# Weight loads, bank waits and emission order in a two-layer diffusion-transformer kernel

## The chip, the cores and the metric

The kernel runs on one core of a Trainium2 chip. A core has TensorE (matrix products, PE in the profile), VectorE (DVE), ScalarE (ACT), GpSimd (POOL), SyncE (SP, which here only issues DMAs) and 16 DMA engines. The engines run their own instruction streams in order and meet only at semaphores. The metric is the device time of one execution in microseconds (us), lower is better; the time before is 1897.44 us, the median of 3 runs (1891.87 to 1897.72).

## The reference

Two layers of a block with three attention branches in parallel, over 512 tokens `x` and 256 context tokens `ctx` of 1024 features; only `x` is returned, so the last layer computes no context output.

```python
def hybrid_layer(x, ctx, c, c_ctx, lw, pos, update_ctx):
    mod_x = silu(c) @ ada_w + ada_b                 # shift, scale, gate
    mod_c = silu(c_ctx) @ ada_w + ada_b
    h  = rmsnorm(x, norm_w) * (1 + scale) + shift   # hc likewise
    p = h @ w_in                                    # 1024 -> 6816 columns
    k_m, v_m, k_s, v_s, k_a, v_a = project_kv(...)  # latents, rope, norms
    q_m, q_s, q_a, z_m, z_s, z_a, g = project_q(...)
    o_m, o_s, o_a = dense MLA, window and dense axial attention, 8 heads each
    y = sum over b of sigmoid(g_b) * ((o_b * silu(z_b)) @ w_o_b)
    x = x + gate * (y @ w_out)                      # ctx likewise if update_ctx

for l in range(2): x, ctx = hybrid_layer(...)
return rmsnorm(x, final_norm_w)
```

## The kernel before

Everything is float32. A product is made of three passes of rounded parts: high x high, high x low, low x high. So each weight chunk (up to 128 x 1024, 512 KB) is loaded by SP into a slot `w_raw`, ScalarE writes `w_hi` (line 1498) and GpSimd writes the rest `w_lo` over the raw data (line 1703); then TensorE may use it. Activations are split likewise: an event `H` on ScalarE writes the high part, an event `L` on VectorE the low part.

A planner, `schedule()`, writes one list of events by hand-made rules, and every engine walks that list in order and takes its own part of each event. A projection is a `group`: an event `G` (the matmuls, line 1273, which alternate between two PSUM banks `acc[0]` and `acc[1]`), an event `E` (reading the bank, on ScalarE, VectorE or both) and, where asked for, `H` and `L`, which the planner puts into a list `later` with a lag; `flush()` empties it at once. A group may start only when the bank's last group has been read. `chunk()` gives each weight the slot that was used longest ago among `usable` slots: three (`TIGHT`) during attention, four (`ROOMY`) elsewhere. The fourth shares memory with attention buffers, so SP waits with it for all value products issued so far (`slot_pv`). The order of the calls of `chunk()` is SP's order of issue, and a wait of SP holds all that is behind it. `split_ahead()` decides where the event `W` of a chunk (both splits) goes.

The stages of a layer, in order: (1) the modulation: rows of `ada_w` are summed by VectorE (`AD`) or, for layer 0's scale, by TensorE with four-row products (`AF`, line 1291); `AC` and `AT` turn the scale row into columns, `VT` transposes the small vectors, `XQ`, `XN`, `XT`, `XM` square, normalise, transpose and modulate the tokens. (2) The latents `ak`, `ckv`, `cq`, `kr` and their sums of squares (`statb`, `statq`). (3) The attention: a loop over pairs of query tiles and heads, with scores into `wide`, softmax, transposes into `ptp`, value products into `pv`; a queue of other groups (the next heads' `mla_head`, the `z` and `y` tiles, queries and keys of the next branch) fills its gaps. (4) Merge: 8 feature tiles, each a gate projection (`g`, then a `tanh` on ScalarE) and the last branch's output projection (`y`), with the rows of `ada_w` for the gate and the next shift in between (`due` says how many after which tile). (5) `wout`: 4 column parts times the token tiles, 24 products of 256 columns each, over all 8 feature tiles.

Ropes use two shared buffers: `swapped` (VectorE shuffles into it, GpSimd multiplies and adds) and `rot`, the result. Before the change each rope's `E` (waits in lines 1785 to 1788) waits until every earlier low part is written, and the planner flushes before it. In `wout` the wait of a group is for all low parts of `y` (`y_ready`, line 795). In `statb` and `statq` TensorE waits for `ev_a=n["ev_a"]`, all reads of ScalarE up to then.

## Time and profile before

| | before |
|---|---|
| median of 3 runs | 1897.44 us (1891.87 to 1897.72) |
| the profiled execution | 1901.16 us |
| its span, first to last instruction | 1899.1 us |
| mean granted TensorE clock | 0.961 |
| TensorE busy | 1744.3 us (92%) |
| VectorE, ScalarE, GpSimd busy | 1086.3, 1048.3, 517.7 us |
| HBM read, mean rate | 121.49 MB, 66 GB/s |

How to read it: the profile is one execution. Its views used here are the page (busy time by engine), the table of waits (for each pair of waiting and releasing operation the idle time in total, how often, and the longest), the timeline (instructions in order of time; in brackets the idle time before an instruction and what ended it) and the table by stretch, in which PEclk is the clock granted to TensorE as a share of 2.4 GHz. A line such as L1273 is the line of the kernel; `acc<-h_hi,w_hi` names what is written and read.

### The profile page before, as it was taken

To read this page: it belongs to the slowest core of one execution; us is meant where nothing else is said; L and a number is where in the kernel's file an instruction comes from. 1 tells how busy PE (TensorE), PEld (TensorE's weight loads), DVE (VectorE), ACT (ScalarE), POOL (GpSimd) and SP (SyncE) were. 2 spreads that over 40 slices of the span, in tenths; PEclk is the share of its full clock that TensorE was granted. 3 is DMA by queue.
4 is the path that set the end of the run, shared out by engine and by line. 5 is a ranking of instruction groups with operands and counts; after the bars stand their busy time and mean duration, and the time that the engine had idled before them with its cause. 6 is when DMAs were issued, how large, how long until landed. Compare 5 with 4: busy or idle time off the path is not lost. (4 is left out here: it accounts for less than half of the span.)

```text
span 1899.1 us, 26967 instructions
## 1 busy us (share of the span) xinstructions
PE 1744.3 (92%) x10544; PEld 1523.4 (80%) x10544; DVE 1086.3 (57%) x2183; ACT 1048.3 (55%) x1915; POOL 517.7 (27%) x296
## 2 busy tenths in 40 slices
PE   7989988999998999998999998978899979999997
PEld 3867877889997889887889976867778867888777
DVE  5533776665555565554756643666565555665534
ACT  3434776666665676754221523766566656776322
POOL 1513212122222222222222432322133222332342
PEclk8998999999999999999999998989999998999899
DMA  8111011011111111114454321111112221211542
GB/s 307 47 24 27 24 32 34 22 40 46 51 46 45 30 49 40 42 37 150 118 165 140 112 60 30 33 30 34 34 45 74 54 61 40 56 51 51 183 133 89
DMA packets 174302, 127.41 MB, mean 67 GB/s; under 512 B 21533, under 2 KB 163423, under 8 KB 174176
## 3 DMA queue, kind: packets, MB, share of 16 engines
q1 hardware_dynamic: 170018, 113.27, 21.1%
q10 hardware_dynamic: 2878, 8.24, 1.2%
q0 software_dynamic: 1280, 4.20, 0.7%
q8 instruction: 83, 1.36, 0.3%
q14 instruction: 43, 0.35, 0.1%
HBM read 121.49 MB, written 4.19 MB: 66 GB/s over the span
## 5 line engine op out<-in xcount | busy, mean ns | idle before, releaser
L1703 POOL TENSOR_TENSOR w_lo<-w_raw,w_hi 128x1024 fp32r<-128x1024 f32 (+4 forms) x188 | 382.5, 2038 | 1217.2 <-ACT w_hi L1498 1216.9
L1273 PE MATMUL acc<-h_hi,w_hi 128*128 128x512 f32 (+2 forms) x1320 | 470.4, 357 | 27.2 <-DVE rot L1798 10.3
L1273 PE MATMUL acc<-h_hi,w_lo 128*128 128x512 f32 (+2 forms) x1320 | 466.1, 354 | 0.0
L1273 PE MATMUL acc<-h_lo,w_hi 128*128 128x512 f32 (+2 forms) x1320 | 462.2, 354 | 0.3 <-POOL h_lo L1741 0.3
L1594 ACT ACTIVATE pt<-ptp 128x512 fp32r<-128x512 f32 (+3 forms) x312 | 166.1, 563 | 271.5 <-PE ptp L1345 270.9
L1887 DVE TENSOR_REDUCE nmax<-wide 128x1 f32<-128x768 f32 (+3 forms) x240 | 189.9, 791 | 208.3 <-PE wide L1325 206.7
L1273 PEld LDWEIGHTS acc<-h_hi,w_hi 128*128 128x128 f32 (+1 forms) x1320 | 251.5, 191 | 68.1 <-issue 16.6
L1273 PEld LDWEIGHTS acc<-h_hi,w_lo 128*128 128x128 f32 (+1 forms) x1320 | 251.1, 190 | 35.0
L1273 PEld LDWEIGHTS acc<-h_lo,w_hi 128*128 128x128 f32 (+1 forms) x1320 | 248.9, 190 | 36.2 <-POOL h_lo L1741 0.5
L1912 DVE TENSOR_TENSOR pt<-ptp,pt 128x512 fp32r<-128x512 f32 (+3 forms) x312 | 192.1, 641 | 54.4 <-ACT pt L1594 54.3
L1586 ACT ACTIVATE e<-e,einv 128x768 f32<-128x768 f32 (+3 forms) x240 | 193.3, 805 | 47.3 <-DVE einv L1904 46.9
L1498 ACT ACTIVATE w_hi<-w_raw 128x1024 fp32r<-128x1024 f32 (+4 forms) x188 | 168.4, 900 | 89.0 <-DMA w_raw<-in_w_out 62.2
L1345 PE MATMUL ptp<-ident,e 128*128 128x128 f32 x1152 | 166.5, 279 | 1.1 <-ACT e L1586 1.1
L1579 ACT ACTIVATE e<-wide,nbias,rq 128x768 f32<-128x768 f32 x160 | 144.9, 906 | 27.1 <-DVE nbias L1893 24.0
L1345 PEld LDWEIGHTS ptp<-ident,e 128*128 128x128 f32 x1152 | 135.1, 143 | 3.2 <-ACT e L1586 1.9
L1325 PE MATMUL wide<-k_s,q_s 128*128 128x256 f32 (+2 forms) x576 | 127.1, 337 | 2.3 <-DVE q_s L1452 1.7
L1358 PE MATMUL pv<-pt,v_s 128*128 128x256 f32 (+1 forms) x384 | 100.3, 288 | 22.6 <-DVE pt L1912 13.6
L1273 PE MATMUL acc<-og_hi,w_hi 128*128 128x512 f32 (+1 forms) x288 | 106.0, 368 | 7.2 <-ACT th_x L1538 7.2
L1273 PE MATMUL acc<-og_lo,w_hi 128*128 128x512 f32 (+1 forms) x288 | 105.3, 366 | 0.0
L1273 PE MATMUL acc<-og_hi,w_lo 128*128 128x512 f32 (+1 forms) x288 | 105.2, 365 | 0.0
L1358 PEld LDWEIGHTS pv<-pt,v_s 128*128 128x128 f32 x384 | 73.5, 191 | 34.1 <-DVE pt L1912 28.8
L1359 PE MATMUL pv<-pt,v_s 128*128 128x256 f32 (+1 forms) x384 | 99.0, 285 | 0.0
(206 smaller groups left out, 3144.4 us busy)
## 6 DMA issues: line engine op xcount, KB each, us to landing
w_raw<-in_w_in SPq DMA_DIRECT2D x102, 512.0 KB, 4.0
w_raw<-in_ada_w SPq DMA_DIRECT2D x48, 512.0 KB, 6.1
w_raw<-in_w_out SPq DMA_DIRECT2D x16, 512.0 KB, 3.5
w_raw<-in_w_o_mla SPq DMA_DIRECT2D x16, 256.0 KB, 2.8
w_raw<-in_w_o_swa SPq DMA_DIRECT2D x16, 256.0 KB, 2.9
w_raw<-in_w_o_ax SPq DMA_DIRECT2D x16, 256.0 KB, 2.8
w_raw<-in_mla_w_uq SPq DMA_DIRECT2D x16, 144.0 KB, 2.4
xres<-in_x SPq DMA_DIRECT2D x2, 1024.0 KB, 16.1
```

What stands on the lines that cost most here:

```text
L1273: ins = nc.tensor.matmul(dst, lhs, rhs, start=first, stop=last)
L1325: ins = nc.tensor.matmul(wide[:, c0:c0 + nk], lhs, rhs, start=(i == 0), stop=(i == len(pairs) - 1 and not masks))
L1345: ins = nc.tensor.transpose(ptp_of(t)[:, b:b + P], e_of(u, c0, c0 + P), ident[:, :])
L1358: nc.tensor.matmul(dst, v_of(pa, kt), pt_of(t, 0)[:, b], start=t["first"] and i == 0, stop=False)
L1359: ins = nc.tensor.matmul(dst, v_of(pa, kt), pt_of(t, 1)[:, b], start=False, stop=t["last"] and i == len(t["blocks"]) - 1)
L1498: nc.scalar.activation(w_hi[s][:, 0:k], w_raw[s][:, 0:k], ACT.Copy).then_inc(w_hi_ready, 1)
L1579: nc.scalar.activation(e_of(u), wide[:, u["lo"]:u["lo"] + u["width"]], ACT.Exp, bias=nbias[:, r:r + 1], scale=scale, accum_out=esum[:, r:r ...
L1586: nc.scalar.activation(e_of(u), e_of(u), ACT.Copy, scale=einv[:, r:r + 1]).then_inc(norm_act, 1)
L1594: nc.scalar.activation(pt_of(t, 0), ptp_of(t), ACT.Copy).then_inc(pt_hi_ready, 1)
L1703: nc.gpsimd.tensor_tensor(w_lo[s][:, 0:k], w_raw[s][:, 0:k], f(w_hi[s][:, 0:k]), ALU.subtract).then_inc(w_lo_ready, 1)
L1887: link(nc.vector.tensor_reduce(nmax[:, r:r + 1], wide[:, u["lo"]:u["lo"] + u["width"]], AX.X, ALU.max, negate=True))
L1912: nc.vector.tensor_tensor(pt_of(t, 1), ptp_of(t), f(pt_of(t, 0)), ALU.subtract).then_inc(pt_lo_ready, 1)
```

## The change

It changes orders and waits; no arithmetic is added but three products that only keep TensorE at work.

- First modulation: the 16 chunks are loaded in another order (shift rows ahead of scale rows), the copy of the small vectors on VectorE (`VC`) moves behind the sixth row, squares and norms of the first two tiles by one row, the first tile's transposes and the shift sums go ahead of `AT`, the second tile's behind it, and three products `KW` are added. The product into `acc[1]` follows the real ones in `AF`.
- Latents: the sums wait for their own squares only, and stand between the query latents 0 and 1 with the rope key before query latent 2; ScalarE's wait in `statb` is for the sum two before.
- Ropes: query heads of the MLA branch (`qm`) and `ak` no longer use `rot`; `qm` writes into `q_f`, the float32 view of its own low part. A rope waits on VectorE only for the low part of the last user of `rot`, and there is a flush only if that one is still due.
- `mla_head` for heads 2, 4, 6: key, value, key, value, query instead of key, key, query, value, value.
- Merge: the chunks of tile t+1 are asked for ahead of the rows behind tile t, and gate chunk 1 is placed while only three slots are usable.
- `wout`: a group waits for feature tile 6 of its own token group, and for tile 7 ahead of its last three products.

```diff
--- before.py
+++ after.py
...
     chunk_last, chunk_at, held, last_used, th_last = {}, {}, [0], [0], {0: None, 1: None}
+    rot_last = [None]
     turn, usable, now, holding = [0], [ROOMY], [0.0], [False]
...
             if g.get("roped"):
-                flush()
-                g["rope_prev"] = (n["rope"], n["l"])
+                if kind not in ("qm", "ak"):
+                    if rot_last[0] is not None and "low_n" not in rot_last[0]:
+                        flush()
+                    g["rot_before"] = rot_last[0]
+                    rot_last[0] = g
+                g["rope_prev"] = n["rope"]
                 n["rope"] += 1
...
         sums, scale = [], []
-        for k in range(KD):
-            sums.append(shift_row(k))
-            scale.append(chunk("adr", 0, 1, k, (0, 1), slot=FIRST[KD + k]))
-            whole.add(scale[-1])
-            used[scale[-1]] = 0
+        for third in (0, 0, 0, 1, 0, 0, 1, 0, 1, 0, 1, 0, 1, 1, 1, 1):
+            if third == 0:
+                sums.append(shift_row(len(sums)))
+            else:
+                scale.append(chunk("adr", 0, 1, len(scale), (0, 1), slot=FIRST[KD + len(scale)]))
+                whole.add(scale[-1])
+                used[scale[-1]] = 0
         early = chunk("win", 0, C_AK, P), chunk("win", 0, C_CKV, P)
...
                 emit("VT")
-            if k == KD // 2 + 1:
+            if k == KD - 3:
+                emit("VC")
+            if k == KD - 2:
                 for tt in (a, b):
...
         emit("AC")
-        for tt in (a, b):
-            turn_rows(tt)
+        turn_rows(a)
+        run_all(shift_sums())
         emit("AT")
+        turn_rows(b)
+        for i in range(2):
+            emit("KW", c=scale[0])
         emit("W", c=early[0])
...
         load_table("s")
-        run_all(shift_sums())
         for tt in (c, d):
...
         turn_rows(c)
+        emit("KW", c=scale[0])
         modulate_rows(b)
...
-    def y_tile(l, b, t, og):
+    def y_tile(l, b, t, og, slots=None):
         branch = BRANCHES[b]
-        cg, cy = chunk("win", l, C_G[branch] + t * P, P), chunk("wo", l, b, t)
+        cg = chunk("win", l, C_G[branch] + t * P, P)
+        usable[0] = slots or usable[0]
+        cy = chunk("wo", l, b, t)
         gates = {tg: project("g", l, cg, tg, branch=branch, t=t, dve=False) for tg in token_groups(l)}
-        ys = [project("y", l, cy, tg, src="og", k=KO, branch=branch, t=t, of=gates[tg], hl=(b == 2), act=False,
+        ys = y_of[l, b, t] = [project("y", l, cy, tg, src="og", k=KO, branch=branch, t=t, of=gates[tg], hl=(b == 2), act=False,
                       needs=lambda: dict(l_done=og[branch])) for tg in token_groups(l)]
...
-    row_of = {}
+    row_of, y_of = {}, {}
...
         go(project("ak", l, ck, "c", roped=False, oldest=ck))
+        squares_ak = n["ev_a"]
         for t in range(KKV):
             go(project("ckv", l, cks[t], "c", t=t))
+        squares_ckv = n["ev_a"]
         load_table("m")
-        for tg in ("x", "c"):
-            go(group("statb", mode="statb", l=l, tg=tg, what="ak", tiles=1, nsum=HD,
-                     needs=lambda: dict(ev_a=n["ev_a"]), rope_done=ropes_ak))
-        for t in range(KQ):
-            c = chunk("win", l, C_CQ + t * P, P)
-            for tg in tgs:
-                go(project("cq", l, c, tg, what="cq", t=t))
-        for tg in ("x", "c"):
-            go(group("statb", mode="statb", l=l, tg=tg, what="ckv", hl=True, tiles=KKV, nsum=KV_RANK, needs=lambda: dict(ev_a=n["ev_a"])))
+
+        def key_sums(tg):
+            go(group("statb", mode="statb", l=l, tg=tg, what="ak", tiles=1, nsum=HD, needs=lambda: dict(ev_a=squares_ak), rope_done=ropes_ak))
+
+        def latent_sums(tg):
+            go(group("statb", mode="statb", l=l, tg=tg, what="ckv", hl=True, tiles=KKV, nsum=KV_RANK, needs=lambda: dict(ev_a=squares_ckv)))
+
+        def query_latents(t, tg, held={}):
+            if tg == "x":
+                held[l, t] = chunk("win", l, C_CQ + t * P, P)
+            if tg in tgs:
+                go(project("cq", l, held[l, t], tg, what="cq", t=t))
+
+        key_sums("x")
+        key_sums("c")
+        query_latents(0, "x")
+        latent_sums("x")
+        query_latents(0, "c")
+        query_latents(1, "x")
+        latent_sums("c")
+        query_latents(1, "c")
         c = chunk("win", l, C_KR, MLA_ROPE)
...
             go(project("kr", l, c, tg, m=MLA_ROPE, width=MLA_ROPE, what="kr", **roped(tg)))
+        for t in range(2, KQ):
+            for tg in tgs:
+                query_latents(t, tg)
         run_all(z_tile(l, 0, 0, zs, og))
...
                 qg += head_q(h + 1, chunk("mq", l, h + 1), 0)
-            return [s for g in (qg + kg + vg if h == 0 else kg + qg + vg) for s in g["steps"]]
+            if h % 2 == 0 and h:
+                return [s for g in (kg[0], vg[0], kg[1], vg[1], *qg) for s in g["steps"]]
+            return [s for g in qg + kg + vg for s in g["steps"]]
...
         sums_at = {3: gate_sums, 6: shift_sums} if l + 1 < LAYERS else {4: gate_sums}
+        tile = y_tile(l, 2, 0, og)
         for t in range(KD):
...
                 merge += step_of(lambda: scale_table(l + 1, V_AXK))
-            merge += y_tile(l, 2, t, og)
-            if t == 0:
-                usable[0] = ROOMY
+            merge += tile
+            if t + 1 < KD:
+                tile = y_tile(l, 2, t + 1, og, slots=ROOMY)
             if t in sums_at:
...
-        y_ready = n["l"]
+        y_low = {(t, g["tg"]): g["low_n"] for t in range(KD) for g in y_of[l, 2, t]}
         gates = n["free"]
...
                     run_all(side_sums())
+                tg = "x" if tt >= TT_CTX else "c"
                 g = go(group("wout", chunk_ids=cc, act=False, cost=cost_of(256, 3 * KD), mode="wout", l=l, j=j, tt=tt, xl=n["xl"],
-                             gates=gates, needs=lambda: dict(l_done=y_ready)))
+                             gates=gates, needs=lambda: dict(l_done=y_low[KD - 2, tg], last=y_low[KD - 1, tg])))
                 if sides and n["xr"] % 2 == 0:
...
     q_m = [shared(f"q_m{i}", [P, 2, TOK], R, at) for i, at in enumerate((51200, 57344, 118784))]
+    q_f = [shared(f"q_f{i}", [P, 2, TOK], F, at) for i, at in enumerate((51200, 57344, 118784))]
     k_m = [shared(f"k_m{i}", [P, 2, TOK], R, at) for i, at in enumerate((63488, 69632, 18432))]
...
                     for i, (dst, lhs, rhs, first, last) in enumerate(mm[a:b]):
+                        if mode == "wout" and a + i == 3 * (KD - 1):
+                            if new(l_done, need["last"]):
+                                pe.wait_ge(l_done, need["last"])
                         if g.get("low_last") and i == 2 * (b - a) // 3:
...
                         pe.wait_ge(raw_load[slot_of[c]], loads[c])
-                    if k < KD - 1:
-                        nc.tensor.matmul(acc[1][0:4, :], cs_n[:, k, :], w_raw[slot_of[c]][:, 0:512], start=True, stop=True)
                     for half in range(2):
...
                         ins.then_inc(af_done, 1)
+                    if k < KD - 1:
+                        nc.tensor.matmul(acc[1][0:4, :], cs_n[:, k, :], w_raw[slot_of[c]][:, 0:512], start=True, stop=True)
+                elif ev == "KW":
+                    if new(row_copied, 1):
+                        pe.wait_ge(row_copied, 1)
+                    nc.tensor.matmul(first_sums(1), cs_n[:, 0, :], w_raw[slot_of[e["c"]]][:, 0:512], start=True, stop=True)
                 elif ev == "AT":
...
+        def rope_out(g, rows):
+
+            if g["kind"] == "ak":
+                return lf[rows, cols("x")]
+            if g["kind"] == "qm":
+                return q_f[g["head"] % 3][rows, 1, cols("x")]
+            return rot[rows, :]
+
         def pieces(g):
...
                 q = q_m[g["head"] % 3]
-                return [(q[0:MLA_K, 0, c], q[0:MLA_K, 1, c], src[0:MLA_K, 0:N])], None
+                got = rope_out(g, slice(0, MLA_K)) if g["roped"] else src[0:MLA_K, 0:N]
+                return [(q[0:MLA_K, 0, c], q[0:MLA_K, 1, c], got)], None
             if what == "km":
...
                     elif kind == "statb":
-                        if new(stat_done, g["stat"] - 1):
-                            act.wait_ge(stat_done, g["stat"] - 1)
+                        if g["stat"] > 2:
+                            if new(stat_done, g["stat"] - 2):
+                                act.wait_ge(stat_done, g["stat"] - 2)
                         ins = nc.scalar.activation(lat_r[:, cols(g["tg"])], src[:, 0:N], ACT.Sqrt, scale=1.0 / g["nsum"], bias=eps_col[:, 0:1])
...
                     rows = slice(0, g["m"]) if g["kind"] != "kr" else slice(MLA_NOPE, MLA_K)
-                    dst = lf[rows, cols("x")] if g["kind"] == "ak" else rot[rows, :]
+                    dst = rope_out(g, rows)
                     if g["kind"] == "kr":
...
-                        if new(rope_done, g["rope_prev"][0]):
-                            dve.wait_ge(rope_done, g["rope_prev"][0])
-                        if new(l_done, g["rope_prev"][1]):
-                            dve.wait_ge(l_done, g["rope_prev"][1])
+                        if new(rope_done, g["rope_prev"]):
+                            dve.wait_ge(rope_done, g["rope_prev"])
+                        if g.get("rot_before") is not None:
+                            if new(l_done, g["rot_before"]["low_n"]):
+                                dve.wait_ge(l_done, g["rot_before"]["low_n"])
                         if new(tab_load, 32 * g["tab"]):
...
                         flip = 8 if kind in ("kr", "qm") else 16
-                        dst = lf[rows, cols("x")] if kind == "ak" else rot[rows, :]
+                        dst = rope_out(g, rows)
                         nc.vector.stream_shuffle(swapped[rows, :], src[pr, 0:N], [i ^ flip for i in range(32)])
...
                     ins.then_inc(ada_used, 1)
-                elif ev == "VT":
+                elif ev == "VC":
                     if new(vec_done, 2):
...
```

## Rows read from the trace of the kernel before

**Rows 1.** The page, first part: busy time and share of each engine.

```profile
PE 1744.3 (92%) x10544; PEld 1523.4 (80%) x10544; DVE 1086.3 (57%) x2183; ACT 1048.3 (55%) x1915; POOL 517.7 (27%) x296
```

**Rows 2.** Waits of TensorE: who waited for whom: total, times, longest (us).

```profile
PE pv L1358 <- DVE pt L1912: 29.9, 26, 3.1
PE pv L1358 <- DVE o_half L1919: 23.9, 16, 2.5
PE acc L1273 <- POOL w_lo L1703: 16.3, 6, 5.9
PE acc L1273 <- DVE rot L1798: 15.5, 6, 4.6
PE acc L1273 <- DVE k_m L1452: 11.9, 6, 3.3
PE acc L1273 <- ACT th_x L1538: 8.3, 5, 3.8
PE acc L1273 <- DVE y_lo L1875: 5.2, 2, 3.2
PE acc L1273 <- ACT lat_r L1520: 3.1, 4, 0.8
PE acc L1273 <- ACT cq_hi L1445: 2.1, 2, 1.3
```

**Rows 3.** Busy time by stretch: length, engines, granted clock (PEclk), DMA share, GB/s.

```profile
897.57:903.03 5.46, 5.46 (x13) 4.30 (x14) 0.00 (x0) 0.65 (x2) 3.05 (x2) 0.50 0.74 248
1773.61:1780.86 7.25, 7.25 (x24) 5.75 (x25) 5.77 (x4) 1.69 (x2) 4.03 (x2) 0.76 0.65 208
124.76:131.98 7.22, 7.22 (x24) 5.71 (x25) 1.80 (x4) 2.43 (x3) 3.26 (x3) 0.76 0.05 13
1004.51:1008.92 4.41, 4.41 (x26) 4.41 (x27) 0.00 (x0) 0.00 (x0) 0.00 (x0) 0.66 0.99 333
1839.57:1845.08 5.51, 5.51 (x26) 5.51 (x27) 0.00 (x0) 1.22 (x2) 4.70 (x2) 0.50 0.24 95
36.00:42.00 6.00, 6.00 (x32) 6.00 (x31) 0.00 (x0) 1.46 (x4) 3.53 (x3) 0.54 0.85 213
```

**Rows 4.** Timeline: start, length, operation; in brackets idle before it and releaser.

```profile
895.88 1.06 ACT L1498 ACTIVATE w_hi<-w_raw 128x1024 fp32r<-128x1024 f32 x1 [6.98 <-DMA w_raw<-in_w_in]
...
1750.46 0.69 DVE L1843 TENSOR_TENSOR y<-y,th_x 128x512 f32<-128x512 f32 x1
...
1773.61 0.56 PE L1273 MATMUL acc<-h_hi,w_hi 128*128 128x512 f32 x1 [2.84 <-POOL w_lo L1703]
```

**Rows 5.** Timeline of POOL, end of layer 1's Merge.

```profile
1835.21 2.37 POOL L1703 TENSOR_TENSOR w_lo<-w_raw,w_hi 128x1024 fp32r<-128x1024 f32 x1 [1.73 <-ACT w_hi L1498]
```

**Rows 6.** Timeline of VectorE, layer 1's first query latent.

```profile
1122.21 0.74 DVE L1454 SCALAR_TENSOR_TENSOR cq_lo<-acc,vec,cq_hi 128x512 fp32r<-128x512 f32 x1
```

**Rows 7.** Timeline of POOL and VectorE, layer 1's first query ropes.

```profile
1164.32 1.29 POOL L1732 TENSOR_TENSOR rot<-rot,swapped 96x512 f32<-96x512 f32 x1
...
1167.16 0.73 DVE L1797 STREAM_SHUFFLE swapped<-acc 96x512 f32<-96x512 f32 x1
```

**Rows 8.** Timeline of VectorE, key pair of layer 1's head 6.

```profile
1286.56 2.27 DVE L1452 TENSOR_TENSOR k_m<-acc,k_m 64x512 fp32r<-64x512 f32 x4 [1.14 <-ACT k_m L1443]
```

**Rows 9.** Timeline of VectorE, ScalarE and TensorE, first modulation.

```profile
18.77 0.21 DVE L1950 COPY vec<-acc 128x54 f32<-128x54 f32 x1 [3.31 <-PE acc L1283]
...
21.59 1.06 ACT L1653 ACTIVATE h_lo<-xres 128x1024 fp32r<-128x1024 f32 x1 [8.71 <-DMA xres<-in_x]
...
24.17 0.59 PE L1291 MATMUL acc<-w_raw,cs_n 128*4 128x512 f32 x1 [0.19 <-DMA w_raw<-in_ada_w]
...
29.44 1.28 DVE L1945 SCALAR_TENSOR_TENSOR w_raw<-w_raw,cs_n,wide 128x1024 f32<-128x1024 f32 x1
...
33.93 1.94 PE L1303 MATMUL pv<-sel,a_row 5*128 5x2 f32 x16
```

**Rows 10.** Timeline of VectorE, first tile of layer 1's Merge.

```profile
1772.44 1.66 DVE L1843 TENSOR_TENSOR y<-y,th_x 128x512 f32<-128x512 f32 x1
```

## The prediction

> **What bounds the kernel now.** I read the page first, then the table of what TensorE waited for, then the timeline of each engine around its longest waits, then the granted clock of the stretches behind them. TensorE is busy for 1744 of 1899 us [rows 1]. So a gain must come out of two places: the 155 us in which it stands still, and the time it works at the lower of its two clock levels. The table of waits [rows 2] sorts the first: 53.8 us are the value product waiting for VectorE inside the attention chain (its first two rows), and no edit here touches those. The others that the change can touch are waits of `acc` groups (line 1273): on POOL's split of a weight (16.3 us, of which one at 1773.61 counts here), on VectorE's rope output `rot` (15.5), on `k_m` (11.9), on ScalarE's `th_x` (8.3), on `y_lo` (5.2), on `lat_r` (3.1) and on `cq_hi` (2.1).
>
> **What a stop costs beyond itself.** Behind a long stop the granted clock is 0.50, which is the 1.2 GHz level, for some five us [rows 3]: 5.46 us after the stop of 3.8 at the start of layer 0's Merge, 5.51 after the stop of 3.2 at the end of layer 1's. I count the loss as (1 - clock) x length: 2.7, 1.7, 1.7, 1.5 and 2.8 us for the first five rows in their order. Taking a stop away should give its clock loss back too, since TensorE worked at 1.00 before these stops; I keep the case that it does not as a rival.
>
> **Merge's start.** Before the change gate chunk 1 takes the fourth weight slot, so SP waits with it for the last value product, and issues it behind rows of 512 KB (two or three). ScalarE meets its split ahead of the `tanh` of gate 0 in its own order and stands there for 6.98 us until the data has landed [rows 4], and TensorE waits 3.8 us for that `tanh` [rows 2]. In layer 1 the same load makes TensorE wait 2.84 us for POOL's `w_lo` [rows 4]. With the change this chunk takes one of three slots; its last user is the final `wo` chunk of the branch before, done some 7 us (layer 0) and 11 us (layer 1) before the attention ends. In layer 1 VectorE adds that last `y` at 1750.46 [rows 4]. The load starts there, with an idle queue, and both splits are done under gate 0. Gain: 3.8 + 2.84 of stops and 2.7 + 1.7 of clock, **11.0 us**. Bounds: 6.6 (stops alone) and 11.0. What is late next: `wo` chunk 1 in the fourth slot, now ahead of the rows, wanted a whole tile later; nothing. SP now also waits for `y` of tile t before it issues the rows behind `wo` t+2; VectorE wants these after tile t+1, 8.8 us (layer 1) to 13 us (layer 0) later.
>
> **Merge's end.** `wout` now waits for feature tile 6 and takes tile 7 only at its last three products of 24. Layer 0: the weights are ready, the stop is 5.2 - 3.2 = 2.0 us [rows 2] and goes whole, with 1.5 of clock [rows 3]. Layer 1: POOL's split of the second `wout` chunk ends at 1835.21 + 2.37 = 1837.6 [rows 5], TensorE began at 1839.57, so only 2.0 of 3.2 go; the remaining 1.2 us stop is short, and I take the clock loss of 2.8 as gone. Sum **8.3 us**, bounds 4.0 and 8.3. Its last-tile wait is covered: 21 products at 0.12 us are 2.5 us, tile 7's low part comes 2 us after the start. Behind it the later `wout` weights are loaded when a pair of slots comes free, so they shift along with the products.
>
> **Latents between sums.** The sums now wait for their own squares, not for the newest of all: `lat_r` 3.1 and `cq_hi` 2.1 go, and so do two of the `rot` stops (2.9 and 2.8, the z tile behind the rope key), because two query groups now lie between [rows 2]. That is 10.9 us, and 1.7 of clock at 124.76 [rows 3]. It adds stops: the next query group wants the bank that VectorE clears with `cq_lo`, and VectorE is behind with the reciprocals of the key sums; in layer 1 it comes to the first `cq_lo` at 1122.21 [rows 6], where the group that wants the bank would be ready about 1 us before. The same stands a second time behind the latent sum. Two per layer, each 0.8 to 1.0 us: minus 3.7. Net **8.9 us**, bounds 4 and 12.
>
> **Ropes of the queries.** Head 1's rope no longer waits for head 0's low part, only for POOL to have done with `swapped`. Layer 1: POOL ends at 1165.61, VectorE began at 1167.16 [rows 7]: 1.5 us; the same in layer 0. **3.0 us**; between 0 and 7, since layer 1 works at 0.50 for some 8 us behind this place and might not.
>
> **Value products between pair keys.** Of the 11.9 us on `k_m`, 10.1 are the four stops of heads 4 and 6 in both layers: the query wants the bank of the first key product while ScalarE copies four pieces and VectorE takes 2.27 us for its four [rows 8]. With 18 small value products (2.1 us) between the two key groups, about 0.5 us of each stop is left, so up to 8 go, and 3 of clock. But ScalarE and VectorE are each busy near three quarters here with work that isn't less, and the two top rows of [rows 2] follow at once. I take half of the stops and half of the clock: **6.5 us**, bounds minus 4 and 12.
>
> **The start.** VectorE stands 3.31 us for the transposed vectors [rows 9]; the copy moves behind the sixth row and this goes. But x now lands three chunks later. Two chunks lie between its landing (21.59) and that of scale chunk 5 (24.17) [rows 9], 1.3 us each: so x at 25.5, and its statistics, which need 4.3 us, at 29.8. VectorE began its last row at 29.44 [rows 9], would now be there at 26.1, and stands until 29.8: all of it is given back. Scale chunk 5 lands at 26.8, so TensorE's last passes end 2.6 us later than before, of which 0.9 fall into a stop that was there. One tile's transposes and the row turn (1.94) [rows 9], 2.9 us together, no longer stand ahead of the shift sums: they begin 1.1 us earlier, but the row turn follows them, and the modulation waits for it: 0.8 us late in all, at the same clock. The stretch from 36 to 42, in which these sums run, was granted 0.54 [rows 3], 2.8 us lost; as the passes end later, most of it may run at 1.00. I take plus 1.0, bounds minus 1.5 and 2. The rest of this stage is a chain over POOL and shifts with it. The three products that keep TensorE busy lie in its waits for `x_mod`.
>
> **Sum**: 11.0 + 8.3 + 8.9 + 3.0 + 6.5 + 1.0 = 38.7 us. The profiled execution took 1901.16 us (2.1 more than its span), 3.7 above the median of the three runs, 1897.44, and above all of them. I set the sum against it, 1901.2 - 38.7 = 1862.5, and say **1862**; against the median it would be 1858.7.
>
> **A rule that speaks against it.** VectorE's add of `y` and `th_x`, both in SBUF, took 1.66 us beside a POOL split [rows 10] and 0.69 without one [rows 4]. The Trainium skill (SBUF — State Buffer, Who interferes with whom) says that a VectorE instruction with two SBUF inputs contends with a GpSimd instruction that reads SBUF; the trace agrees. The change moves the split of gate chunk 1 beside `og_lo`, four such instructions, which end 2.0 us before TensorE needs them in layer 1. If each grew by the 1.0 us of the two rows, `og_lo` would be 2 us late and Merge's start worth 9 instead of 11: 1864.5.
>
> **Rivals.**
> - The clock stays low after the shortened stops (or falls elsewhere). Then only stops are won: 6.6 + 4.0 + 7.2 + 3.0 + 5.0 + 0 = 25.8, **1875**. For it: layer 0's stop of only 2.0 us is followed by 0.66 too. Against: 1.00 wherever groups follow without a stop. 0.12.
> - The attention takes it back: the key stops were cover for ScalarE and VectorE, and the value product waits instead. The pairs cost 4 instead of giving 6.5: **1873**. 0.12.
> - More is won: pairs 12, the ropes with their clock 7, the start 2: **1852**. 0.18.
> - The gate chunk is not early, because its slot's last user ends late or ScalarE meets its split elsewhere: minus 11, **1873.5**. 0.05.
> - Slower: the rows in Merge. They are issued behind a wait for `y`, and VectorE, which works in order, would hold `th_x` and with it every tile. It decides once three rows take longer than one tile, 8.8 us, to land; at 1.3 us a chunk [rows 9] three take 4. Were it so, some 4 us on 14 tiles: 56 us against the 38.7 won: **1918**. 0.03.
>
> The forecast as worked out has 0.50, within 8 us. All rivals but the last are faster by over 0.3% (5.7 us, about what a measurement of this kernel tells from no change); only several of them together reach no change, and I give that 0.03. So faster 0.94, same 0.03, slower 0.03. **Range**: 1848 to 1880, from "more is won" to two of the smaller rivals at once; outside on either side about 0.1.
>
> **What would show it.** In the table of waits: `th_x` down by 3.8, `y_lo` gone or below 1.5 in all, `lat_r` and `cq_hi` gone, new short waits on `cq_lo`, `k_m` below 4; ScalarE's split of gate chunk 1 ahead of the `tanh` without a DMA wait; the clock 1.00 over the first groups of Merge and of `wout`. It is wrong if the rows on `pt` and `o_half` grow by more than 5 us, if x's statistics do not hold VectorE at the seventh row, or if SP's rows land after VectorE asks for them.

## The result, and the profile after

The changed kernel took 1868.24 us (median of four, 1863.98 to 1868.50), the kernel before 1897.58 (median of four): ratio 0.9833 [0.9814, 0.9851], so 29.3 us less. The forecast was 1862, in a range of 1848 to 1880. The profiled execution of the changed kernel was the fastest of its four, 1863.98 us with a span of 1861.9; between the two profiled executions lie 37.2 us, against 38.7 forecast. I show below that this agreement is partly luck.

The table of waits of TensorE after (line waited for: total us, times, longest), which answers [rows 2]:

```profile
engine line waited for: us in total, times, longest us
PE pv L1401 <- DVE pt L1966: 29.7, 27, 3.1
PE pv L1401 <- DVE o_half L1973: 23.6, 16, 2.4
PE acc L1312 <- POOL w_lo L1756: 14.3, 5, 5.9
...
PE acc L1312 <- DVE k_m L1504: 4.9, 3, 2.2
PE acc L1312 <- ACT th_x L1591: 4.0, 4, 1.7
PE acc L1312 <- DVE rot L1852: 4.0, 1, 4.0
PE acc L1312 <- DVE cq_lo L1506: 3.9, 4, 1.7
PE pv L1330 <- DMA w_raw<-in_ada_w: 3.5, 2, 3.1
...
PE acc L1312 <- DVE q_f L1852: 2.3, 3, 1.1
...
PE acc L1312 <- DVE gate L1908: 2.0, 2, 1.7
PE acc L1312 <- DVE v_m L1504: 1.8, 1, 1.8
...
PE acc L1312 <- ACT lat_r L1573: 0.8, 2, 0.4
```

`y_lo` and `cq_hi` are gone, `th_x` is down by 4.3, `rot` by 11.5, `k_m` by 7.0; the two rows of the attention chain stand as they were. New are `cq_lo` (3.9, forecast 3.7), 3.1 us for the first chunk of the modulation, and three that I had not seen coming: `gate` (one of 1.7), `q_f` (2.3, where queries used to wait for `rot`) and `v_m` (1.8, where the value products now stand between the keys).

Of the signs that the prediction named, most came: no DMA wait ahead of ScalarE's split of gate chunk 1, x's statistics hold VectorE ahead of its last two rows (for 1.8 and 1.2 us), no wait of VectorE for a row in Merge. Two did not: `lat_r` is 0.8 and not gone, `k_m` is 4.9 and not below 4.

The windows that answer [rows 3] (us; busy time of each engine; then granted clock, DMA share, GB/s). The first two are the gate groups of Merge's first two tiles in layer 0, the third is `wout`'s start there; the fourth is the first gate group of layer 1, the fifth its `wout`'s start; the last one is the start of the kernel:

```profile
878.11:885.89 7.78, 7.78 (x27) 6.23 (x27) 4.42 (x6) 4.37 (x6) 2.13 (x1) 0.71 0.72 254
892.84:898.47 5.63, 5.63 (x28) 4.67 (x27) 5.53 (x7) 1.89 (x3) 2.40 (x1) 1.00 0.76 258
991.57:997.10 5.53, 5.53 (x50) 5.53 (x49) 2.90 (x7) 1.05 (x2) 0.00 (x0) 1.00 0.54 177
1733.91:1739.55 5.64, 5.64 (x26) 4.32 (x24) 3.35 (x6) 4.04 (x7) 1.32 (x1) 1.00 0.64 225
1804.58:1810.10 5.52, 5.52 (x46) 5.52 (x47) 2.78 (x4) 2.65 (x3) 3.38 (x2) 1.00 0.50 179
36.00:42.00 6.00, 6.00 (x43) 5.58 (x44) 2.21 (x7) 4.27 (x8) 4.68 (x3) 0.80 0.74 191
```

Where [rows 3] had 0.50 to 0.76 behind the stops, both starts of `wout` and the first gate group of layer 1 now run at 1.00. Only the first gate group of layer 0 is at 0.71; the attention's last stop of 1.96 us stands ahead of it, in both kernels.

**The ledger of the two profiles**, by the start times of the same instruction in both:

| term | forecast | measured between the two profiles |
|---|---|---|
| start | 1.0 | 1.0 (71.48 to 70.45) |
| latents | 8.9 | 9.1 (5.7 in layer 0, 3.4 in layer 1) |
| query ropes | 3.0 | 6.1 (0.0 and 6.1) |
| pairs of heads | 6.5 | 2.3 (-0.6 and 2.8) |
| Merge's start | 11.0 | 11.0 (4.7 and 6.4) |
| Merge's end | 8.3 | 7.6 (3.6 and 4.1) |

### The profile page after: what moved, and what is told of

The parts are those of the page before. It is cut to its first block, busy times and chain, and to the rows that moved or that the text cites. A ratio compares the mean times of both kernels' runs of the same rounds, so it can differ in the third digit from the quotient of the medians.

```text
span 1861.9 us, 26973 instructions
## 1 busy us (share of the span) xinstructions
PE 1732.5 (93%) x10550; PEld 1512.3 (81%) x10550; DVE 1088.5 (58%) x2183; ACT 1047.0 (56%) x1915; POOL 518.3 (28%) x296
## 4 chain that ended last, share of the span: by engine, by line
PE 74%; DVE 10%; ACT 8%; POOL 3%; issue 3%; DMA 1%; SPq 0%; DVEq 0%; ACTq 0%; POOLq 0%
PE acc L1312 54%; PE wide L1368 6%; PE ptp L1388 6%; PE pv L1401 4%; PE pv L1402 3%; DVE nmax L1941 2%; DVE pt L1966 2%; ACT e L1632 1%; POOL w_lo L1756 1%; DMA w_raw<-in_ada_w 1%; ACT w_hi L1550 1%; POOL h_lo L1794 1%; DVE k_s L1504 1%; ACT pt L1647 1%; ACT e L1639 1%
```

## The experiments

All ratios are to the kernel before, measured in the same rounds. Six kernels have one part of the change alone, three have all but one or two, one is the changed kernel once more, and two try a cure for the clock. The code is shown in excerpts, with ... where lines are left out.

### One part alone: Merge's start

```diff
...
-            merge += y_tile(l, 2, t, og)
-            if t == 0:
-                usable[0] = ROOMY
+            merge += tile
+            if t + 1 < KD:
+                tile = y_tile(l, 2, t + 1, og, slots=ROOMY)
...
```

> The kernel before with one part alone: Merge prepares its next tile's chunks one tile ahead, so that gate chunk 1 takes the slot of the attention's last wo chunk. My theory (a stop that goes gives back itself and the low clock behind it): 11.0 us less, 5.5 to 6.4 of it in each layer, the ratio near 0.994. Rival (stops alone are won, the clock falls anyway): 6.6 us, ratio 0.9965. Rival (the parts need each other): less than 6. In the profile both long waits at the start of Merge are gone; I also expect one new stop of 1 to 2 us where the gate bank of layer 0 is still held by VectorE at the first sum of rows, as in the kernel with all parts, since that stop stands in this part's own stage.

Measured: 0.9952 [0.9935, 0.9969], 9.1 us less. Both long stops are gone and the new one for `gate` is there. Its cause, in the changed kernel, on VectorE, then POOL, then TensorE (start, duration, line, what, [idle before <- releaser]):

```profile
933.03 2.24 DVE L1929 SCALAR_TENSOR_TENSOR y_lo<-y,y_hi 128x512 fp32r<-128x512 f32 x1
935.20 1.27 DVE L1908 TENSOR_TENSOR gate<-acc,gate 128x512 f32<-128x512 f32 x2
```

```profile
932.38 2.35 POOL L1756 TENSOR_TENSOR w_lo<-w_raw,w_hi 128x1024 fp32r<-128x1024 f32 x1 [3.60 <-ACT w_hi L1550]
```

```profile
936.02 0.47 PE L1312 MATMUL acc<-h_hi,w_hi 128*128 128x512 f32 x1 [1.73 <-DVE gate L1908]
```

Behind this stop the clock stayed at 1.00, here and in the seven other kernels that have the stop:

```profile
936.02:944.50 8.48, 8.48 (x49) 7.49 (x50) 8.13 (x8) 0.60 (x1) 0.00 (x0) 1.00 0.29 114
```

The same `y_lo` in the kernel before, where no split lay beside it:

```profile
945.07 0.68 DVE L1875 SCALAR_TENSOR_TENSOR y_lo<-y,y_hi 128x512 fp32r<-128x512 f32 x1
```

Beside a split of 2.35 us that began first it took 2.24, and the additions that free TensorE's bank came that much later. Layer 1 shows the same without the change: four `y_lo` beside a split took 2.20 to 2.88 us before and four took 2.20 to 2.21 after. So the contention that the prediction weighed is real, but it did not strike `og_lo` (in layer 1 2.50 us for four in both kernels; POOL began 0.4 us before the last was done); what the change added is the one `y_lo` of layer 0.

### One part alone: Merge's end

```diff
...
+                        if mode == "wout" and a + i == 3 * (KD - 1):
+                            if new(l_done, need["last"]):
+                                pe.wait_ge(l_done, need["last"])
...
```

> The kernel before with one part alone: wout waits for feature tile 6 at its start and for tile 7 at its last three products. My theory: 8.3 us less, ratio 0.9956; in layer 0 the stop of 1.94 and the clock loss of 1.5 behind it go, in layer 1 a stop of 1.2 to 1.4 stays, set by POOL's split of the second wout chunk. Rival (stops alone): 4.0 us, ratio 0.998. Everything ahead of the first wout is the kernel before, so the stages there show how much one execution differs from another without any edit: I expect stops of the same length and a clock loss that may differ by up to 2 us a stage.

Measured: 0.9961 [0.9948, 0.9975], 7.4 us less; Merge was 7.6 us shorter than in kernels without the part. In layer 1 of the changed kernel POOL's split of the second `wout` chunk ends at 1804.48 and TensorE starts at 1804.58, which is the bound that the prediction took from [rows 5]:

```profile
1802.12 2.36 POOL L1756 TENSOR_TENSOR w_lo<-w_raw,w_hi 128x1024 fp32r<-128x1024 f32 x1 [1.60 <-ACT w_hi L1550]
```

```profile
1804.58 0.36 PE L1312 MATMUL acc<-w_hi,y_hi 128*128 128x256 f32 x1 [1.36 <-issue]
```

### One part alone: the latents

```diff
...
+        query_latents(0, "x")
+        latent_sums("x")
+        query_latents(0, "c")
+        query_latents(1, "x")
+        latent_sums("c")
+        query_latents(1, "c")
...
```

> The kernel before with one part alone: key sums, latent sums and query latents interleaved, the sums waiting for their own squares only. Ropes still wait for every low part before them. My theory: 8.9 us less, 5.5 in layer 0 and 3.4 in layer 1 (as the stretch from the start of a layer to its query sums showed with all parts), ratio 0.9953; new waits on cq_lo, two in each layer. Rival (the rope wait by the last reader of rot is what took the two rot stops away, not the two query groups between): then a rot stop of 2 to 3 us stays in each layer and only 3 to 5 us are won.

Measured: 0.9960 [0.9945, 0.9976], 7.6 us less; the two stretches of latents and ropes were 9.7 us shorter. The two `rot` stops of 2.9 and 2.8 us behind the rope key went although the ropes waited as before, so it was the latents' part that removed them. About 2.5 us were given back at Merge's start, where the load of gate chunk 1 (behind rows, as in [rows 4]) now cost ScalarE more and TensorE 6.25 us instead of 3.8; with Merge's own part in, this isn't there:

```profile
893.40 1.06 ACT L1528 ACTIVATE w_hi<-w_raw 128x1024 fp32r<-128x1024 f32 x1 [9.87 <-DMA w_raw<-in_w_in]
```

### One part alone: value products between pair keys

```diff
-            return [s for g in (qg + kg + vg if h == 0 else kg + qg + vg) for s in g["steps"]]
+            if h % 2 == 0 and h:
+                return [s for g in (kg[0], vg[0], kg[1], vg[1], *qg) for s in g["steps"]]
+            return [s for g in qg + kg + vg for s in g["steps"]]
```

> The kernel before with one part alone: value products stand between the two key products of a pair of heads. Prediction on record: 6.5 us less. The trace with all parts showed 2.2 us less in the two stretches of mla pairs. Theory A (the clock's luck: the stop of 2.9 in layer 0 went, and a fall of the clock elsewhere, which is not caused by the edit, hid it): this run shows 5 to 8 us less, and the long low stretch of layer 0 is absent. Theory B (the key stops were cover; the attention takes it back, with waits for pt, o_half and a low clock where the 18 small value products have been used up): 0 to 3 us less, and a low stretch of 10 us or more stands again near the same stop for o_half in layer 0.

Measured: 0.9989 [0.9976, 1.0002], 2.1 us less, not told from nothing. Theory B held in its time and in the low stretch; its longer waits for `pt` and `o_half` did not come (29.7 and 23.7, as before). The stretch behind the stop of 2.28 us for `o_half` in layer 0, in the kernel before, the changed one, and this one (granted clock: third number from the end):

```profile
276.19:295.93 19.74, 13.78 (x78) 11.68 (x79) 12.08 (x28) 13.04 (x26) 2.34 (x1) 0.91 0.00 1
```

```profile
268.50:288.24 19.74, 17.71 (x79) 16.07 (x80) 10.51 (x24) 12.61 (x24) 1.97 (x1) 0.57 0.00 1
```

```profile
275.57:295.30 19.73, 17.43 (x95) 15.92 (x96) 11.75 (x27) 13.31 (x26) 2.39 (x1) 0.74 0.00 1
```

TensorE stood 6 us in these 20 before, one half of it for `k_m`, and some 2 now; but the clock was 0.57 and 0.74 where it had been 0.91.

### One part alone: the query ropes

```diff
...
+            if g["kind"] == "qm":
+                return q_f[g["head"] % 3][rows, 1, cols("x")]
...
-                        if new(l_done, g["rope_prev"][1]):
-                            dve.wait_ge(l_done, g["rope_prev"][1])
...
```

> The kernel before with one part alone: the product with the cosine of a query rope goes to a buffer of its own for each head, and the other ropes wait for the last reader of rot only. Prediction on record: 3.0 us less, bounds 0 and 7. From the trace with all parts: layer 0 gave 1.7 and lost it again before the attention, layer 1 gave 6.1, most of it clock. My theory: 3 to 6 us less, ratio 0.997 to 0.998, nothing in layer 0 by the start of the attention. Rival: the layer 1 gain needs the latents' order ahead of it, then 1 to 3 us.

Measured: 0.9985 [0.9968, 1.0002], 2.8 us less, not told from nothing either; its stretches were 1.2 us shorter alone, and 3.9 on top of the latents' order. Nearer to the rival.

### One part alone: the start

```diff
...
+        turn_rows(a)
+        run_all(shift_sums())
         emit("AT")
+        turn_rows(b)
+        for i in range(2):
+            emit("KW", c=scale[0])
...
```

> The kernel before with one part alone: the start (order of the first modulation's chunks, the vectors' copy three rows later, the sums behind one tile's transposes, the three extra products). Prediction on record: 1.0 us less, bounds 1.5 more and 2 less; the stage should end 0.5 to 1.5 us earlier in the profile. Rival (the clock of the first transposes carries on into the latents): 2 to 3 us less by the end of layer 0's latents.

Measured: 1.0015 [1.0002, 1.0028], 2.8 us **more**. Both expectations were wrong. The first products of layer 0 that wait for `h_lo` stood at 70.5 to 71.7 us in the four kernels with this part (mean 71.1) and at 68.8 to 71.5 in the ten without (mean 70.2). The kernel before had been profiled at 71.48, its slowest value; against it the part looked like a gain of 1.0. Where the time goes is on TensorE and VectorE. Without the part (here in the kernel with Merge's end alone) the row turn stood ahead of the two-column sums, and both columns of the modulation are there soon after these:

```profile
33.79 1.94 PE L1310 MATMUL pv<-sel,a_row 5*128 5x2 f32 x16
```

```profile
40.80 0.17 DVE L1865 TENSOR_TENSOR mod_col<-acc,vec 128x16 f32<-128x16 f32 x1 [9.03 <-PE acc L1280]
...
41.02 0.15 DVE L1975 COPY mod_col<-pv 128x16 f32<-128x16 f32 x1
```

With the part (the changed kernel, profiled once more) it stands behind them, here at the lower level of the clock, the modulation waits for it, and the second tile's transposes come behind it:

```profile
38.30 3.57 PE L1346 MATMUL pv<-sel,a_row 5*128 5x2 f32 x16
41.80 1.97 PE L1418 MATMUL ptp<-ident,xn 128*128 128x128 f32 x8
```

```profile
41.91 0.17 DVE L2013 COPY mod_col<-pv 128x16 f32<-128x16 f32 x1 [3.20 <-PE pv L1346]
```

The modulation can begin at 41.9 instead of 41.0 in these two. But single profiles mislead here: this copy stands at 39.7 to 42.4 us in the ten kernels without the part (mean 41.1; 42.42 in the kernel before) and at 40.1 to 42.4 in the four with it (mean 41.5), so 0.4 of the 1.0 us is here. The rest is behind it: from this copy to the products that wait for `h_lo` it takes 29.1 us in each of the ten and 29.4, 29.4, 29.4 and 30.4 in the four. In all four the chain, followed back, goes through the second tile's transposes; without the part (here in the kernel with Merge's end alone) it doesn't. In the three with 29.4 ScalarE's next `xn` waits for them and stands ahead of `h_hi`, in the one with 30.4 VectorE waits for them with its first `x_mod`. That makes 1.0 us in the profiles; the 2.8 of the timed runs has an interval of 0.4 to 5.3.

### All but the pair order, and the changed kernel again

> The changed kernel with the order of value and key products undone, all else kept. Before's order alone gave 2.1 us less [-0.4 to 4.6]. Theory A (the order is worth its stops, a steady 5 us or more): this is 5 us slower than the changed kernel, ratio to before 0.986. Theory B (the stops that it takes away return as clock loss and attention waits): within 2.5 us of the changed kernel, ratio 0.983 to 0.9845. Clock loss over layer 0's attention, first to last value product: the three kernels without this order so far had 8 to 14 us, the two with it 19. If the order causes it, here 8 to 14; if it is chance, this run may show 19 as well.

> The changed kernel itself, once more, on the same chip and in the same rounds as the kernel without the order of value products. Ratio 0.983, as measured. Its second profile says whether layer 0's long low stretch (8.4 us lost between 265 and 285) belongs to it: theory B expects 15 to 20 us of clock loss over layer 0's attention again, theory A 8 to 14.

Measured: 0.9846 [0.9823, 0.9869] without the order of value products, 0.9869 [0.9843, 0.9894] for the changed kernel itself: the order gained nothing here (4.4 us the other way). Layer 0's attention lost 8.5 us to the lower clock without the order and 16.0 with it, as in the changed kernel's first profile (16.0); that is what was expected if the order causes the loss. The two profiles show more (a row of TensorE and the window behind it, without the order first). Up to the first value group of layer 0 TensorE does the same work in both, and meets the same stop; behind it:

```profile
149.99 0.33 PE L1310 MATMUL acc<-w_hi,ckv_hi 128*128 128x128 f32 x1 [2.07 <-DVE k_m L1502]
```

```profile
149.99:159.73 9.74, 9.74 (x62) 8.79 (x63) 3.12 (x6) 2.78 (x4) 0.00 (x0) 1.00 0.30 71
```

```profile
149.22 0.33 PE L1312 MATMUL acc<-w_hi,ckv_hi 128*128 128x128 f32 x1 [2.07 <-DVE k_m L1504]
```

```profile
149.22:163.83 14.61, 14.61 (x62) 13.13 (x63) 3.12 (x6) 2.78 (x4) 0.00 (x0) 0.65 0.19 47
```

The same 62 recorded products took 9.74 us in the one (first two fences) and 14.61 in the other: 4.9 us by the granted clock alone, behind the same stop of 2.07. In layer 1 it was the other way round: that stretch of latents and ropes took 84.4 us without the pair order and 79.2 with it. So with the same work and the same stop the clock falls behind it in one kernel's execution and not in another's. That it is chance isn't shown: the changed kernel, the only one profiled twice, lost 5.1 us behind this stop both times, and nothing at its counterpart in layer 1 both times.

### Two parts undone, the start undone, and stops filled

```diff
...
+                        if mode == "vm" and g["pair"] == 0 and g["tts"][0] == 0:
+                            fill(pv, 256, 10)
+                        if mode == "w" and (g["kind"], g.get("head"), g["tg"]) in (("km", 0, "x"), ("qm", 1, "x")):
+                            fill(pv, 256, 4)
...
+                        if mode == "vs" and g["l"] == 1 and g["tts"][0] == 0:
+                            fill(acc[g["bank"]], 256, 28)
+                        if g["kind"] == "qs" and g["branch"] == BRANCHES[2] and g["head"] == 0 and g["l"] == 1:
+                            fill(acc[g["bank"]], 512, 12)
...
```

Here `fill(bank, width, n)` issues n products of `h_hi` with itself into the bank, and TensorE's wait for the split weights moves behind the filling.

> The changed kernel with two parts undone, the start and the order of value and key products; Merge's two parts, the latents' order and the ropes are kept. Alone, these two parts measured 2.8 us slower and 2.1 us faster, and the changed kernel without the pair order stood within 4 us of the changed kernel. If the parts add up: 1864 to 1867 us, ratio 0.9820 to 0.9835. Rival (the start's order is needed for what follows): 1870, ratio 0.986. In the profile the first stop for h_lo should stand at 68.8 to 71.2, as in the kernels with the start of before.

> The changed kernel with the start alone undone. If the start costs 2.8 us as it did alone: ratio 0.9845 to 0.985 against 0.9869 and 0.9833 of the changed kernel. Rival (nothing: one execution differs from another by more than the start does): within 1 us of it. Clock loss over layer 0's attention: the pair order is in this kernel, so 15 to 17 us again if it causes the loss, 7 to 12 if not.

> The kernel above plus products whose result nobody reads, put where TensorE stands: 10 of 256 columns (1.2 us at 0.12) ahead of head 0's first value group in both layers (stop 2.07), 4 of 256 ahead of head 1's query and of head 0's key group (stops 0.4 to 1.7 for q_f), 28 of 256 (3.4 us) in layer 1's stop of 5.87 for the weights of the swa values, and 12 of 512 (2.8 us) in layer 1's stop of 4.57 for the weights of the first ax query. Theory 1 (the stops themselves lower the granted clock): behind these places the clock stays at 1.00, where the kernels so far lost 3.4 behind the stop of 5.87, 2.5 to 3.5 behind that of 4.57, and 0 to 5 us behind the latents of each layer; 4 to 10 us less than the kernel above, ratio 0.979. Theory 2 (the clock falls by what was done long before, or by chance): the same losses stand at these places, and the time is that of the kernel above or 1 us more.

Measured: 0.9835 [0.9817, 0.9853] with pair order and start undone, 0.9815 [0.9799, 0.9831] with the start alone undone, and 0.9793 [0.9774, 0.9812] filled, 8.0 us less than the first of the three. Between the first two lies the pair order, which now looks worth 3.8 us: with 2.1 alone and 4.4 the other way above, it is nothing that holds. The start undone brought 3.4 us against the changed kernel's first set and 10 against its second, more than either expectation. The loss of clock in layer 0's attention was 13.7 us without the pair order and 14.0 with it, so in this pair the order made no difference to it. The filled stop of layer 0 (TensorE; then the window behind it):

```profile
145.36 1.35 PE L1258 MATMUL pv<-h_hi 128*128 128x256 f32 x10
147.59 0.33 PE L1316 MATMUL acc<-w_hi,ckv_hi 128*128 128x128 f32 x1 [0.88 <-DVE k_m L1504]
```

```profile
147.59:160.00 12.41, 12.41 (x84) 11.44 (x85) 3.82 (x7) 4.66 (x7) 1.47 (x2) 1.00 0.22 56
```

In the five kernels with the latents' and the ropes' part but no filling, 3.4 to 5.2 us were lost behind these stops in 7 of 10 layers; in the two filled ones, in none of 4. In the kernel filled first the stretches of latents and ropes took 178.5 us, against 182.1 to 187.3 in the five (187.3, 8.8 more, in the same kernel without the filling). That is the whole of the gain: behind the stop of 5.87 us in layer 1, of which 2.53 were left, the next 10 us were granted 0.83, against 0.82 unfilled, and the 12 products for the stop of 4.57 stood one group too early.

```diff
...
+                        if g["kind"] == "statq" and g["what"] == "mla" and last and a + i + 1 < len(mm):
+                            fill(pv, 256, 2)
...
```

> The filled kernel with two changes. First, the 16 products that stood one group too early in layer 1 (they met the stop of 4.57 only in part: 1.97 of it stayed, and the group ahead began later) now stand ahead of the gate group that waits for its weights, in its own bank. Second, behind each token tile of the mla query sums (36 products of two columns in layer 0, 24 in layer 1) two unread products of 256 columns are put in, 10 in layer 0 and 6 in layer 1, 1.2 and 0.7 us. In the filled kernel the granted clock fell during these sums (0.62 at 130 to 132 us, 0.50 from 132 to 136) and 3.4 us were lost in each layer. Theory 1 (the clock falls by what TensorE does in the last few us, stops and two-column products alike): both losses of 3.4 go, 6.8 - 1.9 = 4.9 us less, and 1.7 to 3 behind the gate group; ratio 0.9755 to 0.977. Theory 2 (two-column products do not matter, or so few wide ones do not help): the losses stay and the time is 0 to 2 us more, ratio 0.979 to 0.981.

Measured: 0.9807 [0.9787, 0.9827]. Theory 2 held for the two-column sums of the query latents: 3.4 to 5.1 us were still lost in and behind them, with the added products in their way (last columns as above, layer 0):

```profile
129.29:136.44 7.15, 7.15 (x46) 7.07 (x46) 0.42 (x1) 1.25 (x1) 0.00 (x0) 0.72 0.01 2
```

This fall is in every profile: in all 28 layers of the 14 the clock went to 0.50 during these sums or within 0.9 us of their end. In the 16 of these layers that have the latents' part no stop over 0.7 us lies in the 10 us ahead of the sums. In the kernel before (layer 0, from the fall to its end):

```profile
138.90:145.80 6.90, 6.25 (x22) 4.85 (x22) 1.01 (x4) 2.80 (x3) 2.37 (x1) 0.51 0.00 0
```

The gate group's stop was filled and its products ran at 1.00, but the next stop grew (1.6 us in the kernel filled first):

```profile
1530.44 0.79 PE L1316 MATMUL acc<-og_hi,w_hi 128*128 128x512 f32 x1 [3.26 <-ACT th_x L1593]
```

## Why the prediction was right, and where it wasn't

Twelve more profiles give a better ledger than two. Each line is a stage's mean over the kernels without and with a part (in us; both layers together; the kernels with filling left out; low clock is (1 - granted clock) x length over slices of at most 5 us, stops of TensorE in it included):

| stage | without | with | difference | forecast |
|---|---|---|---|---|
| start | 70.2 (10) | 71.1 (4) | +1.0 | -1.0 |
| latents and ropes | 197.7 (5) | 184.1 (5) | -13.6 | -11.9 |
| attention, by the pair order | 1270.7 (8) | 1270.5 (4) | -0.2 | -6.5 |
| its stops | 91.1 | 84.2 | -6.9 | |
| its low clock | 30.2 | 38.8 | +8.5 | |
| Merge, both parts | 358.8 (5) | 339.6 (5) | -19.2 | -19.3 |

(The start's ten include the two filled kernels, whose start is that of before.) The sum is 32.0; the timed runs say 29.3 in one set and 24.9 for the changed kernel's second. A stage without an edit differs by 2.7 to 4.6 us between these profiles, so single profiles could not have settled any term but the two of Merge.

- **Merge** was right, by its own steps: 10.9 for the start alone and 7.6 for the end, against 11.0 and 8.3. The stops gave their clock back, so the rival "the clock stays low" (6.6 and 4.0) is out for these places. Its counter-argument, "1.00 wherever groups follow without a stop", was a misreading all the same: at the two-column sums the clock falls without one. The new stop of 1.7 for `gate` was missed; layer 0 gave 4.7 and not 6.5 for it, and layer 1 gave 6.4 and not 4.5, since the group ahead of the stop also ran at 1.00.
- **The latents** were right (9.7 alone against 8.9): the four stops on `cq_lo` sum to 3.9, as worked out.
- **The ropes** were sized 3.0 and gave 1.2 to 3.9. The stops that went are those forecast (between the two profiles 2.12 us to 0.73 and 2.79 to 1.09, now on `q_f`); the rest of what they are worth seems to hang on whether the clock falls, which no run here settles.
- **The pairs** failed, by the step that took half of the stops and half of the clock as won. (Its 6.5 is half of 10.1 and half of 3; of the 8 us of stops that it says can go, half would have made 5.5.) The stops went (`k_m` 11.9 to 4.9, and 6.9 in all): of the four of heads 4 and 6, layer 0's both to nothing, layer 1's from 3.34 and 2.93 to 1.78 (now on `v_m`) and 2.16, not to 0.5 each. And the rows on `pt` and `o_half` did not grow, so the rival "the attention takes it back" named the wrong way back. It came as clock: layer 0's attention lost 14.0 to 16.1 us to the lower level in four kernels with the order and 6.9 to 13.7 in eight without. I had added clock to the gain where it had to be taken away. That the order lowers the clock rests on these groups and on two of three comparisons with all else alike (7.0 to 15.8 on the kernel before, 8.5 to 16.0 under the changed kernel, but 13.7 to 14.0 with the start undone); by what means stays open: the low stretches lay at other places in each profile.
- **The start** had the wrong sign. The prediction's "0.8 us late in all, at the same clock" was 0.4 in the mean. Its next step, that the stretch from 36 to 42 would mostly run at 1.00, failed: the mean granted clock there is 0.64 in the four kernels with the part and 0.66 in the ten without. So did "the rest of this stage is a chain over POOL and shifts with it": the chain behind became 0.3 to 1.3 us longer. That this looked like a gain of 1.0 came from comparing with one slow profile.
- **The base** was luck. The sum was set against a profiled execution 3.7 us above the median, and this hid part of what the sum had too much: 38.7 us forecast against 29.3 measured between medians, 9.4 too much. With the 32.0 us of the table in place of 38.7 it gives 1869, the median of the kernel before 1866; measured were 1868.

So the forecast was 6.2 us too low, though the sum was 9.4 too high. The terms account for 6.7 of the 9.4: 6.3 in the pairs and 2.0 in the start were too much, 1.7 in the latents and ropes too little. The rest, 2.7, is no more than one stage's spread.

The filled kernel beat the changed one: 1860.7 us against 1868.2 and 1871.1, ratio 0.9793 [0.9774, 0.9812] against 0.9833 [0.9814, 0.9851] and 0.9869 [0.9843, 0.9894]. The one with the start undone (1864.8 us, 0.9815 [0.9799, 0.9831]) is clear of the second set alone. Filling upon the kernel with the start alone undone wasn't tried.

## What to carry to other kernels

A stop of TensorE of about two us costs itself and can cost 3 to 5 us of clock behind it: it did 7 times in 10 ahead of the first values here, and not once in 8 behind the stop of 1.6 to 1.7 for `gate`. Take the stops away whose next groups are seen at the lower level, and where one can't go, try products in it that nobody reads, in a free bank and shorter than the stop. Stops taken out of the attention chain won nothing here, 6.9 us of them against 8.5 more of low clock: count the clock behind a change and not only the stops. And a term under some 4 us wants several profiles on either side: compare stage by stage, with all kernels that share the stage.

## What the runs showed of the hardware

- The granted clock fell to 1.2 GHz behind a stop of 2.07 us in one kernel's execution and stayed at 2.4 GHz in another's, with the same work ahead of it. The Trainium skill (TensorE: Matmul & The Clock Gate, Part 1) describes what watches TensorE's activity as free-running, not started by the program; by that rule a stop's place against it is chance. These two traces agree; the two of the changed kernel, which fell at the same stop, neither bear it out nor refute it.
- TensorE's clock fell to 1.2 GHz in or right behind the two-column sums of the query latents in all 28 layers profiled, 16 of them with no stop over 0.7 us in the 10 us ahead.
- With unread products in the stops ahead of the first values the clock was 1.00 behind them in 4 of 4 layers, without them in 3 of 10; the same kind of products, two by two among two-column sums, did not keep it (0.72 over 7.15 us).
- A VectorE instruction with both inputs in SBUF took 2.24 us instead of 0.68 when it began 0.65 us into a POOL split of 2.35; it ended 0.54 us behind that split. The Trainium skill (SBUF — State Buffer, Who interferes with whom) names such a pair as contending; the trace agrees, and puts 1.6 us on this case.
